# A two-layer diffusion backbone on one core: input-outermost first tiles and projections, and another order in the odd block

## What is computed

```
def half_ffn(h, mod, j, w, g, b, alpha):
    y = swiglu(modulate(h, mod, j), *w)          # (silu(m @ w_gate) * (m @ w_up)) @ w_down
    return layer_norm(alpha * h + 0.5 * gate(mod, j) * y, g, b)
...
# mixer:  h <- LN(a*h + g_1 * W_out[mixers(mod_1(h) W_in)])
# even layer: neighbourhood attention heads | bidirectional mLSTM heads
# odd layer:  bidirectional S5 channel groups | bidirectional retention heads
def s5_out(y, u):
    y = jax.nn.gelu(y + d_skip * u)
    return y * jax.nn.sigmoid(y @ glu_w + glu_b)     # the gated unit
...
ret_l = jax.nn.silu(pl[4]) * head_norm(rl, gn_w)     # retention, with its gates
```

## Time and profile before

| | |
|---|---|
| median of 3 runs | 2232.83 us (2228.66, 2232.83, 2236.64) |
| the profiled execution | 2227.38 us, its span 2225.7 us |
| granted TensorE clock, mean over the span | 0.944 of 2.4 GHz |
| PE busy | 1971.9 us, 89% |
| DVE busy | 1338.0 us, 60% |
| ACT busy | 633.2 us, 28% |
| POOL busy | 314.6 us, 14% |

### The profile page before, as it was taken

One profiled execution on the slowest core, in us unless ns is written; L12 is line 12 of the kernel. 1 busy time (PEld: TensorE's weight loads), 2 busy tenths in 40 slices (PEclk: granted clock), 3 DMA queues, 4 the chain that ended last, 5 costly groups with the idle time before them and its releaser, 6 DMA issues. The chain is left out here.

```text
span 2225.7 us, 22816 instructions
## 1 busy us (share of the span) xinstructions
PE 1971.9 (89%) x8568; PEld 1467.3 (66%) x8568; DVE 1338.0 (60%) x2145; ACT 633.2 (28%) x1015; POOL 314.6 (14%) x326
## 2 busy tenths in 40 slices
PE   0999999879999885969999996999999798778997
PEld 0788878634554442448887884888778356668996
DVE  7677776352855677176778627775577443345454
ACT  0322233122333321132224213222333410413452
POOL 0000001140000010330000114000035433222003
PEclk9999999989998987979999997999999899888998
DMA  7355535132430000135554322544224644203543
GB/s 291 129 212 185 192 146 149 66 116 82 147 137 1 1 0 0 42 121 196 188 188 166 119 112 80 215 177 170 95 106 173 242 147 175 76 1 114 186 149 119
DMA packets 43952, 290.02 MB, mean 130 GB/s; under 512 B 13916, under 2 KB 19676, under 8 KB 27232
## 3 DMA queue, kind: packets, MB, share of 16 engines
q1 hardware_dynamic: 34336, 270.08, 33.1%
q10 hardware_dynamic: 9536, 18.88, 2.3%
HBM read 272.16 MB, written 16.78 MB: 130 GB/s over the span
## 5 line engine op out<-in xcount | busy, mean ns | idle before, releaser
L514 PE MATMUL bank<-m_hi,w_hi 128*128 128x512 f32 (+1 forms) x1408 | 326.9, 372 | 104.2 <-ACT m_hi L919 104.2
L1378 DVE CUSTOM_DVE_ANT_0 L<-slot 128x1024 f32<-128x1024 f32 x288 | 356.4, 1238 | 84.4 <-DMA slot<-in_ada_dram 63.6
L933 ACT ACTIVATE w_hi<-slot 128x1024 fp32r<-128x1024 f32 x176 | 186.3, 1061 | 605.7 <-PE bank L521 592.4
L514 PEld LDWEIGHTS bank<-m_hi,w_hi 128*128 128x128 f32 x1408 | 247.9, 192 | 160.2 <-issue 89.9
L1417 DVE TENSOR_TENSOR w_lo<-slot,w_hi 128x1024 fp32r<-128x1024 f32 x176 | 217.0, 1235 | 225.8 <-ACT w_hi L933 219.8
L518 PE MATMUL bank<-m_lo,w_hi 128*128 128x512 f32 (+1 forms) x1408 | 314.4, 366 | 0.0
L521 PE MATMUL bank<-m_hi,w_lo 128*128 128x512 f32 (+1 forms) x1408 | 311.5, 364 | 0.0
L518 PEld LDWEIGHTS bank<-m_lo,w_hi 128*128 128x128 f32 x1408 | 247.2, 192 | 41.8
L521 PEld LDWEIGHTS bank<-m_hi,w_lo 128*128 128x128 f32 x1408 | 245.0, 190 | 41.3
L1528 DVE TENSOR_TENSOR down_lo<-slot,down_hi 128x1408 fp32r<-128x1408 f32 x64 | 108.7, 1710 | 135.2 <-ACT down_hi L980 134.9
L553 PE MATMUL bank<-g_lo,down_hi 128*128 128x512 f32 (+1 forms) x704 | 152.4, 365 | 0.1
(11 more groups left out here) (304 smaller groups left out, 2490.7 us busy)
## 6 DMA issues: line engine op xcount, KB each, us to landing
slot<-in_gateup_dram SPq DMA_DIRECT2D x44, 2048.0 KB, 7.8
slot<-in_ada_dram SPq DMA_DIRECT2D x36, 2048.0 KB, 7.8
slot<-in_down_dram SPq DMA_DIRECT2D x32, 1408.0 KB, 6.0
slot<-in_ev_in_dram SPq DMA_DIRECT2D x4, 2048.0 KB, 9.1
slot<-in_od_in_dram SPq DMA_DIRECT2D x4, 2048.0 KB, 9.7
R<-s_ops SPq DMA_DIRECT2D x16, 512.0 KB, 5.3
s_tables<-slot ACTq DMA_DIRECT2D x8, 768.0 KB, 3.3
R<-s_tables SPq DMA_DIRECT2D x8, 768.0 KB, 5.2
```

The source lines that it names most:

```text
L514: nc.tensor.matmul(bank[j][:, c0:T], w_hi[:, off, c, :], m_hi[:, c, c0:T], start=(c == 0), stop=False)
L933: nc.scalar.activation(w_hi[:, off, :, :].rearrange("p a b -> p (a b)"), slots[b][:, (2 * (f % 2) + off) * D:(2 * (f % 2) + off + 1) * D], ...
L1378: ins = nc.vector.tensor_tensor_reduce(out=junk, in0=slots[k][:, t * D:(t + 1) * D], in1=csilu[s_], scale=1.0, scalar=0.0, op0=ALU.mult, o ...
```

## The change

Five things are written in another order; no arithmetic is added or left out.

1. First tiles of the four feed-forward stages: `first_tile` runs over the inputs outermost. It waits first for both `w_lo` parts, then does for each input c, as it comes, hi x hi and hi x lo of the gate and of the up tile (banks 0 and 2), with the `m_lo` products three inputs (gate) and five inputs (up) behind, and the rest of these at the end.
2. First projections of both mixers (`project_first`): for each input four output tiles, in banks 0 to 3.
3. Output projections: output tiles 0 to 3 are done together, input after input, in the banks 5, 6, 4, 7; then tiles 4 to 7 one after the other as before.
4. Attention bias: tiles 0 to 3 are flipped on PE between ffn0's last down matmul and its norm statistics, and masked by DVE ahead of the norm; tiles 4 to 7 keep their place. The first projection waits for four masks, and the gates' product behind it for all eight.
5. Odd block: the order of the projections is u, k, q, v, gates. k's first two tiles come ahead of the scan's first inputs, one tile goes into each batch (two into batches 2 and 3), and the four gate tiles come behind the rotary products. On ACT gelu is ahead of the gates' silu, and the decays are behind it. The gated unit comes behind retention, its halves before and after the head means. SP loads q ahead of v, and one load more ahead of the ring.

```diff
-ODD_LOADS = [(0, "od_in", 0, SLOT), (1, "od_in", 1, SLOT), (2, "od_v", None, SLOT), (3, "od_in", 2, SLOT),
-             (0, "od_in", 3, SLOT), (1, "glu", None, HEADS * WIDTH), (2, "od_out", 0, SLOT), (3, "od_out", 1, SLOT)]
+ODD_LOADS = [(0, "od_in", 0, SLOT), (1, "od_in", 1, SLOT), (3, "od_in", 2, SLOT), (2, "od_v", None, SLOT),
+             (0, "od_in", 3, SLOT), (1, "glu", None, HEADS * WIDTH), (3, "od_out", 1, SLOT), (2, "od_out", 0, SLOT)]
...
+        def proj_out(d):
+            return (banks[5], banks[6], banks[4], banks[7])[d] if d < 4 else out_bank[d % 2]
...
                     odd_load()
                     odd_load()
+                    odd_load()
                     ring_inputs(2)
...
-                        if b in (2, 3, 5, 7):
+                        if b in (2, 5):
                             odd_load()
+                    odd_load()
...
+                def first_tile():
+                    unit = s * 2 * FT + 2
+                    take(0)
+                    pe.wait_ge(sem("w_lo_ready"), unit)
...
+                    late = (3, 5)
+                    for c in range(KT):
+                        pe.wait_ge(m_ready, before("m_ready", name) + c + 1)
+                        for off in range(2):
+                            nc.tensor.matmul(acc[off][:, c0:T], w_hi[:, off, c, :], m_hi[:, c, c0:T], start=(c == 0), stop=False)
+                            nc.tensor.matmul(acc[off][:, c0:T], w_lo[0][:, off, c, :], m_hi[:, c, c0:T], start=False, stop=False)
+                        if c >= late[0]:
+                            pe.wait_ge(sem("m_lo_ready"), s * KT + c - late[0] + 1)
+                        for off in range(2):
+                            if c >= late[off]:
+                                lo(off, c - late[off])
+                    for off in range(2):
+                        for c in range(KT - late[off], KT):
+                            pe.wait_ge(sem("m_lo_ready"), s * KT + c + 1)
+                            last = lo(off, c)
+                        last.then_inc((gate_done, up_done)[off], 1)
...
+                first_tile()
+                pair(0, 0, None, (1,))
...
+                if s == 0:
+                    pe.wait_ge(sem("even_params_in"), 16 * 8)
+                    pe.wait_ge(sem("na_bias_in"), 16 * ROWS * ROWS)
+                    for n in range(4):
+                        turn_bias(n)
                 norm_stats(name, c0)
...
+                take(slot_pair[0])
+                for c in range(KT):
+                    pe.wait_ge(sem(f"{name}_y{c // 4}"), c % 4 + 1 if c >= 4 or name == "odd" else 2 * (c + 1))
+                    for d in range(4):
+                        last = nc.tensor.matmul(proj_out(d)[:, c0:T], wslot(slot_pair[0])[:, d, c, :], y[:, c, c0:T],
+                                                start=(c == 0), stop=(c == KT - 1))
...
+                take(slot_pair[1])
+                for d in range(4, KT):
+                    pe.wait_ge(sem("r_ready"), before("r_ready", name) + (d - 3 if d < 6 else d - 1))
...
+            def project_first(name, k, into):
+                take(k)
+                for c in range(KT):
+                    pe.wait_ge(sem("m_ready"), before("m_ready", name) + c + 1)
+                    for j in range(4):
+                        last = nc.tensor.matmul(into[j][:, :], wslot(k)[:, j, c, :], m[:, c, :], start=(c == 0), stop=(c == KT - 1))
...
-                for n in range(8):
-                    nc.tensor.matmul(banks[n][:, :], flip[:, :], bias_flipped[:, n // 4, 2 * (n % 4):2 * (n % 4) + 2, :]
-                                     .rearrange("p a b -> p (a b)"), start=True, stop=True).then_inc(sem("na_bias_turned"), 1)
-                pe.wait_ge(sem("na_bias_masked"), 8)
-                project("even", 0, 0, False)
+                pe.wait_ge(sem("r_ready"), before("r_ready", "ffn0") + KT)
+                for n in range(4, 8):
+                    turn_bias(n)
+                pe.wait_ge(sem("na_bias_masked"), 4)
+                project_first("even", 0, banks[0:4])
...
-                    pe.wait_ge(sem("odd_proj_read"), k + 1)
+                    pe.wait_ge(sem("odd_proj_read"), 2 * b + 2 if b < 2 else k + 1)
...
-                for j in range(4):
-                    proj_tile(j, 0, False)
-                    if j >= 2:
-                        inputs(j - 2)
+                project_first("odd", 0, banks[0:4])
                 pe.wait_ge(sem("odd_params_in"), 16 * 9)
...
+                proj_tile(*next(ahead))
+                proj_tile(*next(ahead))
+                inputs(0)
+                inputs(1)
                 for b in range(len(BATCHES)):
+                    for _ in range(2 if b in (2, 3) else 1):
+                        proj_tile(*next(ahead))
                     if b + 2 < len(BATCHES):
                         inputs(b + 2)
-                    proj_tile(*tiles[2 * b])
-                    proj_tile(*tiles[2 * b + 1])
                     outputs(b)
...
+                for tile in ahead:
+                    proj_tile(*tile)
...
+                glu(0)
+                glu(1)
+                head_means("odd", CTX)
+                glu(2)
+                glu(3)
+                head_variances("odd", CTX)
+                pe.wait_ge(sem("glu_read"), 4)
                 out_proj("odd", (2, 3), CTX)
...
                 for n in range(20):
+                    if n == 16:
+                        act.wait_ge(sem("s5_y_done"), len(BATCHES))
+                        gelu(0)
+                        gelu(1)
...
+                decays()
+                gates(0)
+                gates(1)
+                head_squares("odd", CTX)
+                gates(2)
+                gates(3)
+                head_deviations("odd", CTX)
...
+                if s == 0:
+                    mask_bias(0, 4)
                 norm(n, name, c0)
```

151 lines of the change are left out of this document (78 added, 73 removed).

## The result

The changed kernel takes 2199.0 us (median of 2193.8, 2198.3, 2199.7 and 2200.8) against 2234.1 for the kernel before on the same chip: ratio 0.984, 95% interval 0.982 to 0.987, so 35 us faster. The forecast was 2191 in a range from 2179 to 2204, so the result is inside the range and 8 us above the forecast: 35 us were gained where 42 were added up. Two terms of the sum were too small, and the trace says which.

What follows compares the result with a forecast made beforehand. PE, busy 1971.9 of 2225.7 us, was taken as the bound, with gains where it waits or runs at its low clock. Terms -11.5 - 18.4 - 7.2 - 7.1 - 4.5 + 3.8 + 3 = -42 took 2232.8 to 2191 us, range 2179 to 2204.

Steps and rivals of the forecast that it cites:

- rival A: Odd's scan loop runs cold, PE falling back to clock 0.50 and setting the step: 2200 us (2197 to 2207), chance 0.12.
- rival B: First tiles stay at the low clock; ffn1, ffn2 and ffn3 gain 3 each: 2201 us (2197 to 2205), chance 0.08.
- signs of being wrong: Scan steps above 16 us, clock 0.50 for a whole first tile, or a new wait in even behind the gates' product.
- Even's entry: First projection starts at 453.7, not 465.18, and keeps its 29.62 us: gain 11.5, bounds 8 and 12.
- Even's output: Output projection of even ends at 924.4 in place of 942.8: gain 18.4, bounds 16 and 19.
- The first tiles: Gains of 7.2 in ffn1, 7.1 in ffn2, 4.5 in ffn3; high clock expected about half way.
- ffn0: First tile waits for both w_lo parts ahead of all 48 matmuls: loss 3.8, bounds 3 and 6 (cold start of 2.1).
- Odd, the scan: Later start, then steps of 15.3 us a batch: scan late by 8, 9 at most, 4 if PE stays warm.
- Odd, behind the scan: Gelu's end to weighting again 12.5; reciprocals late by 15; output projection gains 12.3; odd in sum +3, bounds -4 and +9.
- Rival D: Slower than before through table loads lengthening scan steps; 20.3 at each of six means +30, 2221 us; chance with the rest 0.03.
- Rival C: Better than forecast: gated unit hides in odd's head norm, scan stays warm, odd -4: 2184 us, chance 0.09.
- rival E: Upstream gains vanish because what follows waits for something else, such as a weight load; half lost: 2212 us, chance 0.04.

Runs made afterwards that it cites:

- experiment 6: Changed kernel with the first tiles of ffn1, ffn2 and ffn3 put back to the old order: 2218.3 us, ratio 0.993.
- 7: Changed kernel with even's output projection put back, tile by tile: 2213.6 us, ratio 0.993.
- 9: Changed kernel with even's entry put back (eight bias tiles and masks together, first projection tile by tile): 2207.7 us, ratio 0.989.
- experiment 1: Changed kernel with ffn0's first tile alone put back to its old order: 2192.0 us, ratio 0.982.
- experiment 2: Changed kernel with the odd block and its loads put back, except that its output projection stays input-outermost: 2177.3 us, ratio 0.976.
- experiments 3: Changed kernel with only the start of odd's scan put back (u tile by tile, first inputs between, no k tile ahead): 2199.2 us, ratio 0.984.
- 5: Changed kernel with the start of odd's scan and the order of the load queue put back: 2177.7 us, ratio 0.976.
- experiment 8: The kernel of experiment 2 with the big loads inside the scan issued right behind table loads, the last behind the loop: 2171.8 us, ratio 0.973.
- 11: The kernel of experiment 8 with a new first tile in ffn0, products with w_lo at the end: 2165.3 us, ratio 0.969.
- Experiment 10: The changed kernel itself, run again unaltered: 2200.5 us, ratio 0.984.

## Why the prediction was right, point by point

*The number and the mechanism.* By its number alone 2199 would fit rival A (2200) and rival B (2201) better than the forecast (2191). The traces rule both out, as said below. The 8 us between are terms and places that came out otherwise, +2.1 in ffn0, +3.1 in odd, +2.7 ahead of odd, +2.5 in ffn3, -1.8 in even's middle and -0.5 in even's output and ffn1's first tile. Three of them, ahead of odd, in ffn3 and in even's middle, were not in the working at all; that the sum of all stayed inside the range is in part luck. Of the signs of being wrong that the prediction named one came, once: a step of the scan above 16 us.

*What is shown.* Put back one at a time, the parts cost 19 (first tiles, experiment 6), 19 (even's output, 7) and 10 (entry, 9), and give 5 (ffn0, 1) and 19 (odd's order, 2). The 12.0 of odd's output projection are read from the landmarks of experiment 2, not from a kernel without it. That makes 19 + 19 + 10 + 12 - 5 - 19 = 36, and 35 were measured. The parts add, as far as single ones are known (some 4 us each by their intervals).

*Even's entry* was sized right, 11.5 in the trace, but not by one term: the wait for the masks gave 11.35, the norm's statistics behind the four early bias tiles ran 0.9 shorter, and the first projection took 0.7 more, 30.36 against the 29.62 that it was to keep. *Even's output* too, 18.7 against 18.4, with the last group, tile 4 and POOL's sums as described. *The first tiles* came to 7.4, 7.1 and 4.5 against 7.2, 7.1 and 4.5. In ffn1 the low clock held for the first two of the eight inputs and the matmuls took 0.23 us from 938.7 on, with the third input and so sooner than "about half way"; it made no difference, since ACT's `w_hi` was the last to come. Rival B is out. (Its gain of 3 for a tile that is cold all through was 2.4 by its own working, 984.47 - 982.07.)

*ffn0*: right mechanism, and the term was mis-sized, +5.9 in place of +3.8. The working took 48 matmuls of 0.227 from 67.2 on. In the trace nine stand in the first four us and 17 in the next four, and the first ten took 0.43 each, which makes 2.0 of the 2.1 more. The bound "6 (with a cold start of 2.1)" was the value. The sum counted the high speed from the first matmul on; the granted clock of 1.00 in that stretch would not have warned, and the earlier trace rows are silent on it. A line of the kernel before that they don't show is not: there eight matmuls took 2.74 us, over 0.3 each.

```profile
64.63 2.74 PE L518 MATMUL bank<-m_lo,w_hi 128*128 128x512 f32 x8
```

*Odd, the scan*: 8 forecast, "9 at most", 9.2 measured. The start was 1.6 better than worked out (second rotation 47.9 behind the first matmul, 49.6 forecast), and the step of 18.0 took that back, so the nearness of the two numbers is luck in part. "The load that made one step 20.3 now lies elsewhere" was right for that load; another one took its place. What the prediction didn't see at all is how much loads and scan hang together: it put the order of the queue at nothing, and experiments 3 and 5 differ by 18 us through the queue alone. The late start covers it in the changed kernel.

*Odd, behind the scan*: "again 12.5" from gelu's end to the weighting was the step that failed. It is 15.0 (1894.3 to 1909.3), against 12.8 before: the second pair of gate tiles waits 5.0 us for ACT's table load and silu, starts at a clock of 0.50, and takes 9.71 in place of 7 to 8.5. So the weighting is late by 11.8, not 8. The gated unit in the head norm costs 6.3 against 6.9, and the output projection gives 12.0 against 12.3. In sum +6.1 in place of +3, inside the bounds.

*Rival A* saw the right thing and gave it the wrong price. In the loop the outputs of every second batch, four in all, run at the low clock, wholly or but for the first matmuls (1769 to 1774 at a granted clock of 0.50). The Trainium skill, "TensorE: Matmul & The Clock Gate", section "HAM oscillation — how this bites in real kernels", says that bursts of matmuls with idle time between them are each begun at the low clock. The trace agrees for three of the four; the one at 1832.57 began high and was low after 1 us. But PE had waited 3.3 to 7.9 us for POOL's states ahead of each of them, so the lost speed came out of waiting time and the steps stayed at 15.0 to 15.2. *Rival D*'s mechanism occurred once in the changed kernel (+2.8), and to avoid it was worth 5 us of the scan in experiment 8. *Rival C* is out, since odd lost 6.1 us in place of gaining 4, and so is *rival E*: the gains upstream stand in every later landmark.

*Unforeseen*: 1.8 us less in even's middle, 2.7 more around ffn2's down projection and norm (a slower restart behind a 3.0 us wait that the kernel before has too, and the 1.1 ahead of odd) and 2.5 more in ffn3. The 1.8 are no gain of the change: from even's first projection to its head means this one profile took 393.8 us, and those of experiments 1 to 11 took 396.7 to 402.4. Experiment 10 shows that such amounts come and go between executions of one kernel. I don't explain them further.

## What to carry to other kernels

When a projection or a first tile has to wait for inputs one by one, run over the inputs outermost in as many banks as there are. It was worth what a count of the matmuls behind the last input says, in five places of this kernel (three first tiles, two output projections); in even's first projection it was changed together with the masks and has no number of its own. But look for operands that are late as a whole (here `w_lo`) and put their products last. Before work in front of a chain of latencies is reordered, write down the queue that feeds the chain: a small load that the chain needs must stand ahead of big loads and of loads that wait for something. And a sum that comes out right doesn't clear its parts: here one of five parts cost 18 us while the whole gained 35.

## What the runs showed that I had not expected

- The granted clock can read 1.00 while matmuls take 0.43 us, twice their 0.227: from 67 to 71 in the changed kernel, and in all runs within the first 10 us of PE's work (3.59 us for eight matmuls in experiment 1). At a program's start the durations tell the speed, not that column.
- A table load of 768 KB is taken up by the rotation 4.4 us behind its issue, 7.2 when issued 0.8 us behind a load of 1 MB, and 9.9 when issued 1 us behind one of 2 MB. A load of 2 MB issued 3.3 us behind it did no harm (4.3), nor did one 0.4 us behind it in experiment 8 (4.1).
- Executions of one kernel differ by up to 10 us (2191.4 to 2201.2) with nearly the same waits; in the two that have a trace the difference is made in the sparse middle of even, where the clock stands at 0.50 for longer in one. A part of 5 us needs the ratio over many executions, or its own landmarks in the trace.
